# Attention outputs rooted, scaled and turned head by head into the rows of the output product, with two output slabs split early

## The chip, the cores and the metric

One Trainium2 chip, one core, one launch. The metric is the device time in microseconds (us) of the launch. Engines are named as in the profile: PE is the TensorE matmul, PEld its weight load, DVE is VectorE, ACT is ScalarE, POOL is GpSimd, SP is SyncE, whose queue carries the weight loads. A time written 675.2 is a position in the profiled span, in us from its start.

## What is computed

The program is a transformer block followed by two layers of a second kind, on 256 tokens plus 256 context tokens, all float32. In each of the two layers the attention reads:

```python
def diff_attend(q, k, v, lam):
    s = jnp.einsum('bqhcd,bkhcd->bchqk', q, k).astype(jnp.float32) * (ATT_HEAD_DIM ** -0.5)
    p = jax.nn.softmax(s, axis=-1)
    a = p[:, 0] - lam * p[:, 1]
    return jnp.einsum('bhqk,bkhe->bqhe', a.astype(v.dtype), v)
...
def post(o):
    return (rmsnorm(o, subln_g) * (1.0 - lam_init)).reshape(o.shape[0], o.shape[1], ATT_V_DIM)
...
def merge(att, ssd, ga, gs):
    return (jax.nn.sigmoid(ga) * (att @ w_attn_o) + jax.nn.sigmoid(gs) * ssd) @ w_out
```

There are 8 heads of 128 output features. The change concerns `post` (a root mean square over each head of 128, a gain, a constant), the turn of its result from tokens to features, the product `att @ w_attn_o`, and what runs beside it: the step sizes `dt` of the scan (a product of the layer's input with 64 columns of `w_in`, a bias and a softplus) and the sums of `dt * a` over a chunk, from which the scan's decays come.

## The kernel before, in words

**Products in parts.** A float32 product is made as three products of rounded parts: high weights by high input, high weights by low input, low weights by high input. So each slab of weights (128 partitions x 2048 words, 1024 KB, which is 256 output columns by 8 tiles of 128 inputs) is rounded to a high part, and the rest is written over the slab in the ring. In layer 0 POOL does both steps (`split`: L2712 for the high part, L2689 for the rest, each in 4 pieces of 512 words); in layer 1 ACT rounds (`round_slab`, L1368) and POOL takes the rest (`rests`). Both raise `split_ready`, on which PE waits in `split_weights`.

**The ring.** All weights pass a ring of 4 slots. SP issues the loads in the order of use and waits for each until the slab four places earlier has been used (`done[slab - SLOTS]`). Ahead of the output product the ring carries the "mod" slabs (rows of `ada_w`, 1024 KB each, 24 of them in layer 0 and 12 in layer 1), which PE multiplies inside the attention, one per unit at most, where the table `mods_of` puts them (`spread`: over all 32 units of layer 0, over all 16 of layer 1). After the mods come the slab of `dt`, four slabs of `w_attn_o`, and the first slabs of the scan.

**The attention.** A unit is one head and one tile of 128 queries (32 in layer 0, 16 in layer 1; in layer 0 units of 512 and of 256 keys take turns). Per unit u, PE makes the scores of u+2 (L1022), turns the weights of u (L926), makes the outputs of u-1 (L1034) and, where there is one, a mod product (L655). DVE takes the maximum (L2318), scales the outputs of two units before (`out2`, L2339) and mixes the two softmaxes (L2326, L2329, L2333). ACT makes the exponentials (L1611), copies the turned weights (L1465) and squares the outputs, four units behind (L1620).

**After the attention.** ACT takes one root over all heads (L1634); DVE inverts it (L2357), multiplies by `1 - lam_init` (L2359) and scales the outputs, one instruction for each tile of tokens (L2364, 128x1024). Meanwhile PE makes the `dt` product (`to_tokens`, L762: 4 tiles). Then PE turns all 8 heads (L842), with ACT (L1392) and DVE (`rest_of_turned`, L2035) taking the high and the low part of each, and runs a `fill` (L776, matmuls without a result). Then comes the output product, 8 tiles of 128 features (L704, each 8 input tiles by 3 parts = 24 matmuls); behind tiles 4, 5, 6 and 7 PE makes the decay sums of one tile of tokens (`decay_sums`, L1072). DVE multiplies each tile by its gate (`merge`, L2398). ACT and DVE work through the softplus of `dt` beside it (L1654 to L1660, L2370 to L2389); ACT then rounds the first slabs of the scan (`round_of_group(0, q)`, L1651) and takes the exponentials of the decay sums (L1670):

```python
for t in range(TT):
    if t == TT - 1:
        round_of_group(0, 2)
    act.wait_ge(*c.need(dec_ready))
    act.activation(edec[:, t, :], PS[:, 4 + t, 0:192], ACT.Exp)
```

POOL takes the rests of those slabs and then stops at `stage`, where PE, ACT, DVE and POOL wait for one another (`rest_of_group`, L2759; POOL's drain, L2659). Behind it PE begins the scan (L1106).

**To_features by rows.** `to_features` has a form with `row_ready`: its first four tiles (two slabs) are not made one after the other but side by side in four PSUM banks, input tile by input tile ("row" by row), and before each row `row_ready` is called. It is used elsewhere in the kernel.

## Time and profile before

| | us |
|---|---|
| median of 3 runs | 2586.83 (2586.74 to 2587.83) |
| the profiled execution, its own time | 2582.65 |
| its span | 2580.8 |
| PE busy | 2497.3 (97%) |
| POOL busy | 1494.0 (58%) |
| DVE busy | 1217.4 (47%) |
| ACT busy | 1125.7 (44%) |

The profile is of one execution. Its span is the time between the first and the last instruction; the execution's own time has 1.85 us more, and the median of the runs shown is 4.18 us above that. Busy time of one engine may lie beside that of another, so the shares don't add up. The profile's chain of waits is walked back from the last instruction, at each step to what released it.

### The profile page before, as it was taken

The numbers are of one execution on the slowest core, as the hardware profiler recorded it, in microseconds if no ns is written. First come the engines' busy times: TensorE is split into PE (matmuls) and PEld (weight loads), VectorE is DVE, ScalarE is ACT, GpSimd is POOL, SyncE is SP. The second block draws the span as 40 slices with busy tenths as digits, with TensorE's granted clock in tenths as the row PEclk, the third lists the DMA queues.
The fourth block names the chain that finished last, engine by engine and source line by source line (L and its number), as shares of the span: only waits on it lengthen the run. The fifth ranks groups of instructions, "written<-read, shape, count | busy, mean of one in ns | idle before, by whom it ended". The sixth has DMA issues, their size and how long they took to land.

```text
span 2580.8 us, 39739 instructions
## 1 busy us (share of the span) xinstructions
PE 2497.3 (97%) x15548; PEld 2180.7 (84%) x15548; DVE 1217.4 (47%) x2583; ACT 1125.7 (44%) x2371; POOL 1494.0 (58%) x1318
## 2 busy tenths in 40 slices
PE   8999999999999999999999999999989999889999
PEld 7779998985788888888888888889868888889998
DVE  3635502327747888873342112122464888743210
ACT  2445433116527776763032011042465666544532
POOL 1019775860355555544966888854234657656976
PEclk9999999999899999999999999999999999999999
DMA  7566463328432222215323333332544322264564
GB/s 211 195 180 180 127 168 101 95 85 293 157 108 75 58 66 74 58 50 164 98 66 109 94 94 97 97 115 82 183 140 123 91 79 82 77 173 139 184 173 115
DMA packets 388969, 313.03 MB, mean 121 GB/s; under 512 B 12576, under 2 KB 374082, under 8 KB 387778
## 3 DMA queue, kind: packets, MB, share of 16 engines
q1 hardware_dynamic: 385874, 297.75, 39.0%
q10 hardware_dynamic: 2352, 12.59, 1.3%
q8 instruction: 109, 1.79, 0.3%
q0 software_dynamic: 576, 0.43, 0.2%
q14 instruction: 58, 0.48, 0.1%
HBM read 303.40 MB, written 7.34 MB: 120 GB/s over the span
## 4 chain that ended last, share of the span: by engine, by line
PE 72%; POOL 10%; DVE 8%; issue 6%; DMA 2%; ACT 2%; POOLq 1%; SPq 0%; DVEq 0%; ACTq 0%
PE PS L704 34%; POOL rounded L2689 10%; PE PS L1106 10%; PE PS L762 5%; PE PS L1113 3%; PE PS L727 2%; DVE mid_a L2432 2%; PE PS L1234 2%; PE PS L1147 2%; PE PS L655 2%; PE PS L1156 2%; PE PS L1034 1%; PE PS L926 1%; PE PS L1022 1%; DVE mid_v L2486 1%
## 5 line engine op out<-in xcount | busy, mean ns | idle before, releaser
L2689 POOL TENSOR_TENSOR rounded<-ring,rounded 128x512 fp32r<-128x512 f32 (+1 forms) x872 | 1113.1, 1309 | 746.6 <-ACT rounded L1368 424.9
L704 PE MATMUL PS<-rounded 128*128 128x256 f32 (+1 forms) x6864 | 1139.0, 328 | 11.7 <-ACT xT L1758 6.8
L704 PEld LDWEIGHTS PS<-rounded 128*128 128x128 f32 x6864 | 1020.6, 191 | 124.0 <-issue 8.7
L2712 POOL TENSOR_TENSOR rounded<-ring,constants 128x512 fp32r<-128x512 f32 x216 | 229.3, 1092 | 246.9 <-PE PS L704 123.9
L1106 PE MATMUL PS<-rounded 128*128 128x512 f32 (+1 forms) x1536 | 343.5, 380 | 5.6 <-DVE mid_a L2432 5.1
L1106 PEld LDWEIGHTS PS<-rounded 128*128 128x128 f32 x1536 | 275.3, 188 | 60.8 <-DVE mid_a L2432 3.7
L1368 ACT ACTIVATE rounded<-ring 128x2048 fp32r<-128x2048 f32 (+1 forms) x99 | 180.0, 1822 | 150.4 <-DMA ring<-in_w_mlp_dram 55.2
L2432 DVE SCALAR_TENSOR_TENSOR mid_a<-PS,V,mid_a 128x510 f32<-128x510 f32 (+3 forms) x256 | 182.2, 714 | 25.6 <-ACT mid_a L1697 18.1
L1735 ACT ACTIVATE rounded<-constants,big 128x128 fp32r<-128x128 f32 x384 | 150.3, 391 | 0.0
L1735 ACT ACTIVATE rounded<-constants,mid_v 128x128 fp32r<-128x128 f32 x384 | 150.2, 391 | 0.0
L1113 PE MATMUL PS<-rounded 128*128 128x256 f32 x1152 | 147.8, 286 | 0.0
L1113 PEld LDWEIGHTS PS<-rounded 128*128 128x128 f32 x1152 | 142.6, 191 | 1.8
L1907 ACT ACTIVATE PS<-PS 128x512 f32<-128x512 f32 (+1 forms) x64 | 30.4, 475 | 251.4 <-DVE PS L2620 251.3
L2597 DVE SCALAR_TENSOR_TENSOR xT<-PS,mod,xT 128x256 f32<-128x256 f32 x40 | 17.9, 481 | 244.4 <-PE PS L704 244.4
L2620 DVE TENSOR_SCALAR PS<-PS 128x512 f32<-128x512 f32 (+1 forms) x64 | 36.1, 566 | 188.1 <-PE PS L704 177.9
L2469 DVE SCALAR_TENSOR_TENSOR big<-big,by_head 128x128 f32<-128x128 f32 x192 | 106.1, 611 | 18.4 <-POOL big L2790 18.1
L1651 ACT ACTIVATE rounded<-ring 128x1024 fp32r<-128x1024 f32 (+1 forms) x64 | 93.1, 1476 | 32.0 <-DMA ring<-in_w_in_dram 32.0
L762 PE MATMUL PS<-rounded 128*128 128x256 f32 x768 | 102.7, 290 | 0.0
L2305 DVE TENSOR_TENSOR edec<-PS,constants 128x256 f32<-128x256 f32 x32 | 13.6, 425 | 179.1 <-PE PS L1006 178.8
L762 PEld LDWEIGHTS PS<-rounded 128*128 128x128 f32 x768 | 96.4, 191 | 1.8
L727 PE MATMUL PS<-rounded 128*128 128x256 f32 (+1 forms) x480 | 87.0, 341 | 5.7 <-DVE rounded L2041 4.0
L727 PEld LDWEIGHTS PS<-rounded 128*128 128x128 f32 x480 | 75.1, 191 | 17.4 <-DVE rounded L2041 3.8
(263 smaller groups left out, 3114.5 us busy)
## 6 DMA issues: line engine op xcount, KB each, us to landing
ring<-in_w_mlp_dram SPq DMA_DIRECT2D x64, 1024.0 KB, 5.6
ring<-in_w_in_dram SPq DMA_DIRECT2D x56, 1024.0 KB, 5.3
ring<-in_ada_w_dram SPq DMA_DIRECT2D x48, 1024.0 KB, 5.2
ring<-in_w_in_dram SPq DMA_DIRECT2D x81, 512.0 KB, 4.1
ring<-in_w_up_dram SPq DMA_DIRECT2D x44, 512.0 KB, 5.1
ring<-in_w_ssd_o_dram SPq DMA_DIRECT2D x16, 1024.0 KB, 5.8
ring<-in_w_out_dram SPq DMA_DIRECT2D x12, 1024.0 KB, 5.1
ring<-in_w_down_dram SPq DMA_DIRECT2D x16, 704.0 KB, 4.9
```

The lines of the kernel that those rows point to most:

```text
L704: mm = pe.matmul(PS[:, b, 0:cols], w[:, k, m * P:(m + 1) * P], x(half * kt + k), start=(half == 0 and k == 0 and n_pass == 0), stop=(half ...
L727: mm = pe.matmul(PS[:, b, 0:cols], w[:, k, m % 2 * P:(m % 2 + 1) * P], x(k), start=(k == 0 and n_pass == 0), stop=(k == kt - 1 and n_pass ...
L762: mm = pe.matmul(PS[:, b, 0:width], x[:, k, t * P:(t + 1) * P], w[:, k, :], start=(k == 0 and n_pass == 0), stop=(k == KT - 1 and n_pass = ...
L1106: mm = pe.matmul(PS[:, b, 0:cols], w[:, k, m:m + P], x[:, k, 0:cols], start=(k == 0 and x is hs_hi and w is w_hi), stop=(k == KT - 1 and w ...
L1113: mm = pe.matmul(PS[:, b, t * GW:(t + 1) * GW], x[:, k, t0:t0 + P], w[:, k, :], start=(k == 0 and x is hs_hi and w is w_hi), stop=(k == KT ...
L1368: act.activation(view(R, at[n % len(at)], size), ring[:, slab % SLOTS, 0:size], ACT.Copy)\
L1651: act.activation(view(R, group_hi(s, q), words), ring[:, s, 0:words], ACT.Copy).then_inc(*c.made(round_ready))
L1735: act.activation(seg_parts[d][n][:, r * P:(r + 1) * P], mask, ACT.Copy, scale=dta_parts[n][:, t, h:h + 1]).then_inc(*c.made(seg_in))
L2432: ins = dve.scalar_tensor_tensor(out=cv[:, :, to], in0=u[:, :, fr], scalar=V[:, bass.ds(g * st + (cw + 32 * (d + 2) + off), 1)], in1=cv[:, ...
L2469: step(dve.scalar_tensor_tensor(out=m, in0=cb_lo[:, t, :], scalar=dt[:, t, g * GH + r:g * GH + r + 1], in1=m, op0=ALU.mult, op1=ALU.add))
L2689: ins = pool.tensor_tensor(lo[:, r], raw[:, r], hi[:, r], ALU.subtract)
L2712: ins = pool.tensor_tensor(hi[:, r], raw[:, r], ones[:, 0:1].broadcast_to([P, 512]), ALU.mult)
```

## The change

- **Roots.** ACT takes the root in two parts: over the first 7 heads in layer 0 (6 in layer 1) in the last unit of the attention, over the rest after it (`roots_of_heads`). The factor `1 - lam_init` is multiplied into the gain once, at the start.
- **Scaling and turning by head.** DVE scales head by head over all tiles of tokens (`scale_head`, 128x512 in layer 0, 128x256 in layer 1): heads 0 and 1 before the outputs of the last unit, each later head ahead of the low part of the head two before. PE turns heads 0 and 1 and then makes the first four tiles of the output product side by side (`row_ready=head_row`): before row f it turns head f+2 and waits for the low part of head f.
- **dt.** The `dt` product is made behind these four tiles (`between`), and its slab is loaded between the second and the third slab of `w_attn_o`. All four decay sums move behind the last two tiles: t=0 and 1 behind tile 6, t=2 and 3 behind tile 7.
- **Mods.** The mod products are spread over the first 26 of the 32 units of layer 0 and the first 13 of the 16 of layer 1.
- **Slabs.** In layer 0 POOL splits the first two slabs of `w_attn_o` inside the attention, as soon as they are loaded, into memory of their own (`split_into`). In layer 1 ACT rounds them in units 14 and 16, the third after the turned heads, the fourth behind the first four `hs_hi` copies (L1658).
- **DVE.** `merge` of the first four tiles comes ahead of the softplus, the other four behind it, each with two rests of `hs_lo`.

```diff
+        out_at = [[AT["big2"] + KT * T, AT["big2"] + KT * T + SLAB], mix_at[1][0:2]]
...
-        mods_of = [spread(len(UNITS1), 0, EARLY), spread(len(units2(0)), EARLY, LATE + EARLY),
-                   spread(len(units2(1)), 2 * EARLY + LATE, LATE)]
+        mods_of = [spread(len(UNITS1), 0, EARLY), spread(len(units2(0)) - 6, EARLY, LATE + EARLY),
+                   spread(len(units2(1)) - 3, 2 * EARLY + LATE, LATE)]
+        rooted_first = [HEADS - 1, HEADS - 2]
...
+                first_slab["attn_o", l] = len(done)
+                wide(of_layer("w_attn_o_2", l), 0, 2)
                 slabs(1, KT, 64, lambda j: wi[:, :, C_DT:C_DT + 64], lambda j: TT * j)
-                first_slab["attn_o", l] = len(done)
-                wide(of_layer("w_attn_o_2", l), 0, 4)
+                wide(of_layer("w_attn_o_2", l), 512, 2)
...
-                pe.wait_ge(*c.need(o_done))
-                ring_begin(dve_freed)
-                to_tokens(1, 64, TT, dve_freed)
-                pe.wait_ge(*c.need(tok_scaled, n_tok))
-                turn_begin()
-                for f in range(KT):
-                    turn([o2[:, t, f * P:(f + 1) * P] for t in range(n_tok)])
-                fill(3, tile[0] % 4)
-                turn_end()
+                def turn_head():
+                    f = heads_turned[0]
+                    if f == KT:
+                        return
+                    heads_turned[0] += 1
+                    if f == 1:
+                        pe.wait_ge(*c.need(o_done))
+                    pe.wait_ge(*c.need(tok_scaled))
+                    turn([o2[:, t, f * P:(f + 1) * P] for t in range(n_tok)], ring=False)
+
+                def head_row():
+                    turn_head()
+                    pe.wait_ge(*c.need(turned_freed))
                 def decay_sums(n):
-                    t = n - 4
-                    if t < 0:
+                    if n < 6:
                         return
-                    if t == 0:
+                    if n == 6:
                         pe.wait_ge(*c.need(dta_ready))
+                    for t in (2 * n - 12, 2 * n - 11):
...
+                for _ in range(2):
+                    turn_head()
                 to_features(4, lambda k: att_hi[l][:, k, :], q_cols, dve_freed, rest=lambda k: att_lo[l][:, k, :],
-                            hi_at=mix_at[l], after=decay_sums, begin=False)
+                            hi_at=mix_at[l], after=decay_sums, row_ready=head_row, first_at=out_at[l],
+                            between=lambda: to_tokens(1, 64, TT, dve_freed))
...
+                    if u == n_u - 1:
+                        roots_of_heads(0, rooted_first[l])
+                    if l and u in (n_u - 2, n_u):
+                        round_slab(slabs, 16 + (u - n_u + 2) // 2, mix_at[l])
-                act.activation(stat[:, 224:224 + ny * HEADS], stat[:, 192:192 + ny * HEADS], ACT.Sqrt, scale=1.0 / P,
-                               bias=eps[:, 0:1]).then_inc(*c.made(tok_rms))
-                if l:
-                    for n in range(16, 20):
-                        round_slab(slabs, n, mix_at[l])
+                roots_of_heads(rooted_first[l], HEADS)
                 for f in range(KT):
                     turned_to(att_hi[l][:, f, :], q_cols, col("attn_subln_g_2", l), hi_ready)
+                if l:
+                    round_slab(slabs, 18, mix_at[l])
...
                 for k in range(KT // 2):
                     act.activation(hs_hi[:, k, :], hT[:, k, :], ACT.Copy).then_inc(*c.made(hi_ready))
+                if l:
+                    round_slab(slabs, 19, mix_at[l])
                 act.wait_ge(*c.need(dt_one))
...
+                    if u == n_u + 1:
+                        roots_taken(0, rooted_first[l])
+                        for f in range(2):
+                            scale_head(f)
-                for t in range(ny):
-                    h = o2[:, t, :].rearrange("p (h e) -> p h e", h=HEADS)
-                    dve.tensor_tensor(h, h, bc(stat[:, 192 + t * HEADS:192 + (t + 1) * HEADS], P), ALU.mult)\
-                        .then_inc(*c.made(tok_scaled))
+                for f in range(2, KT):
+                    if f == rooted_first[l]:
+                        roots_taken(f, HEADS)
+                    scale_head(f)
+                    rest_of_head(f - 2)
+                for f in range(KT - 2, KT):
+                    rest_of_head(f)
+                for n in range(4):
+                    merge(n)
...
-                for n in range(KT):
-                    merge(n)
-                    rest_of(hs_lo[:, n, :], hT[:, n, :], hs_hi[:, n, :])
+                for n in range(4):
+                    merge(4 + n)
+                    for k in (2 * n, 2 * n + 1):
+                        rest_of(hs_lo[:, k, :], hT[:, k, :], hs_hi[:, k, :])
...
+                    a0 = first_slab["attn_o", l]
+                    pool.wait_ge(*slab_used[s0 + 15])
+                    for n in range(2):
+                        split_into(a0 + n, out_at[l][n])
                     pool.wait_ge(*c.need(o_done, len(units2(l))))
-                    split(range(a0, a0 + 4), mix_at[l])
+                    for n in range(2):
+                        split_into(a0 + 3 + n, mix_at[l][n])
...
-                    rests(range(a0, a0 + 4), mix_at[l])
+                    rests([a0, a0 + 1, a0 + 3, a0 + 4], mix_at[l])
```

## Rows read from the trace of the kernel before

**Rows 1.** The page, part 1: busy time, share, instructions.
```profile
PE 2497.3 (97%) x15548; PEld 2180.7 (84%) x15548; DVE 1217.4 (47%) x2583; ACT 1125.7 (44%) x2371; POOL 1494.0 (58%) x1318
```

**Rows 2.** Timeline of PE, layer 0: start, extent, group, idle before it.
```profile
675.62 12.63 PE L762 MATMUL PS<-ring,hT 128*128 128x64 f32 x64 [0.44 <-DVE mid_o L2339]
...
695.66 27.51 PE L704 MATMUL PS<-rounded 128*128 128x512 f32 x120 [0.68 <-DVE rounded L2035]
...
737.26 5.74 PE L704 MATMUL PS<-rounded 128*128 128x512 f32 x24
742.84 1.22 PE L1072 MATMUL PS<-by_head,constants 128*128 128x32 f32 x10
...
746.31 18.90 PE L1106 MATMUL PS<-rounded 128*128 128x512 f32 x82 [0.15 <-POOLq L2659]
```

**Rows 3.** Windows: stretch, busy PE, PEld, DVE, ACT, POOL, granted clock, DMA, GB/s.
```profile
677.00:690.60 13.60, 13.60 (x67) 13.60 (x67) 12.06 (x12) 1.92 (x4) 13.52 (x10) 0.50 0.09 27
1916.00:1922.80 6.80, 3.90 (x14) 3.24 (x15) 3.42 (x8) 6.52 (x11) 6.80 (x6) 0.51 0.01 2
```

**Rows 4.** Timeline of PE, layer 1.
```profile
1903.60 7.36 PE L762 MATMUL PS<-ring,hT 128*128 128x64 f32 x64 [0.45 <-DVE mid_o L2339]
1910.80 1.04 PE L842 MATMUL PS<-constants,mid_o 128*128 128x128 f32 x8
1918.90 1.97 PE L842 MATMUL PS<-constants,mid_o 128*128 128x128 f32 x8 [7.06 <-DVE rounded L2035]
...
1922.87 14.77 PE L704 MATMUL PS<-rounded 128*128 128x256 f32 x120
...
1949.43 1.22 PE L1072 MATMUL PS<-by_head,constants 128*128 128x32 f32 x10
...
1955.28 13.00 PE L1106 MATMUL PS<-rounded 128*128 128x512 f32 x56 [0.38 <-POOLq L2659]
```

**Rows 5.** Timeline of PE in the attention of layer 0: turned weights of units.
```profile
595.33 0.66 PE L926 MATMUL PS<-constants,big 128*128 128x128 f32 x4 [0.50 <-DVE big L2333]
...
601.32 0.66 PE L926 MATMUL PS<-constants,big 128*128 128x128 f32 x4
...
606.87 0.66 PE L926 MATMUL PS<-constants,big 128*128 128x128 f32 x4 [0.50 <-DVE big L2333]
...
667.27 0.44 PE L926 MATMUL PS<-constants,big 128*128 128x128 f32 x2
...
672.62 0.44 PE L926 MATMUL PS<-constants,big 128*128 128x128 f32 x2 [0.36 <-DVE big L2333]
```

**Rows 6.** Timeline of POOL, layer 0: one slab's high part; another's rest.
```profile
675.64 4.03 POOL L2712 TENSOR_TENSOR rounded<-ring,constants 128x512 fp32r<-128x512 f32 x4 [109.85 <-DVE mid_o L2339]
...
692.63 5.00 POOL L2689 TENSOR_TENSOR rounded<-ring,rounded 128x512 fp32r<-128x512 f32 x4
```

**Rows 7.** The instructions of line L2364 (DVE): duration ns min/median/max.
```profile
L2364 DVE TENSOR_TENSOR mid_o<-mid_o,stat x6: 1218/2144/2286, 678.7 to 1907.3; 128x1024 f32<-128x1024 f32 x6
```

**Rows 8.** Timeline of DVE, attention of layer 0.
```profile
669.35 0.75 DVE L2333 SCALAR_TENSOR_TENSOR big<-big,stat 128x512 f32<-128x512 f32 x1
```

**Rows 9.** The page, part 6: issues, KB each, us from issue to landing.
```profile
ring<-in_ada_w_dram SPq DMA_DIRECT2D x48, 1024.0 KB, 5.2
```

**Rows 10.** Timeline of ACT, layer 0, at the last tiles of the output product.
```profile
737.49 0.33 ACT L1670 ACTIVATE edec<-PS 128x192 f32<-128x192 f32 x1 [6.28 <-PE PS L1072]
737.72 1.91 ACT L1651 ACTIVATE rounded<-ring 128x2048 fp32r<-128x2048 f32 x1
```

**Rows 11.** The chain of waits, layer 0: POOL's last rest and its drain.
```profile
739.67 6.60 POOLq L2659
```

**Rows 12.** Timeline of ACT, layer 1: table load of the root; softplus.
```profile
1904.00 1.28 ACT L1634 ACT_TABLE_LOAD   x1
...
1921.28 0.41 ACT L1654 ACTIVATE big<-big 128x256 f32<-128x256 f32 x1
...
1923.33 2.18 ACT L1658 ACTIVATE rounded<-hT 128x512 fp32r<-128x512 f32 x4
```

More of the change, by code:

```diff
@@ L672, in to_features @@
                             rest=None, hi_at=None, lo_at=None, after=None, row_ready=None, first_at=(None, None), aside=4, first_rows=None,
-                            begin=True, end=True, held=None, last_rows=None):
+                            begin=True, end=True, held=None, last_rows=None, between=None):
                 if begin:
@@ L735, in to_features @@
                     side_by_side()
+                    if between:
+                        between()
                     for j in range(aside // 2, 4):
@@ L1052, in _ @@
                 c.skip(p_ready, 4)
[L1053 to L1055 removed]
                 n_tok = len(y_chunks(l))
[L1057 to L1062 removed]
+                heads_turned = [0]
@@ L1073, in decay_sums @@
-                    mm.then_inc(*c.made(dec_ready))
+                    for t in (2 * n - 12, 2 * n - 11):
+                        for m, lhs, r0, w in ((0, t_gt, 0, 32), (32, t_le, 0, 32), (64, t_lt, 32, 32), (96, t_ge, 32, 32),
+                                              (128, ones, 0, 64)):
+                            mm = pe.matmul(PS[:, 4 + t, m:m + w], lhs, dta[:, t, r0:r0 + w], start=True, stop=True)
+                        mm.then_inc(*c.made(dec_ready))
+                for _ in range(2):
+                    turn_head()
@@ L1548, in _ @@
                 a0 = first_slab["attn_o", l]
-                slabs = [*range(s0, s0 + 16), *range(a0, a0 + 4)]
+                slabs = [*range(s0, s0 + 16), a0, a0 + 1, a0 + 3, a0 + 4]
                 if l == 0:
@@ L1621, in sum_squares, with roots_of_heads @@
                                    accum_out=stat[:, 192 + t * HEADS + h:193 + t * HEADS + h]).then_inc(*c.made(act_step))
+                def roots_of_heads(h0, h1):
+                    act.wait_ge(*c.sofar(act_step))
+                    roots, sums = (stat[:, at:at + ny * HEADS].rearrange("p (t h) -> p t h", h=HEADS)[:, :, h0:h1]
+                                   for at in (224, 192))
+                    act.activation(roots, sums, ACT.Sqrt, scale=1.0 / P, bias=eps[:, 0:1]).then_inc(*c.made(tok_rms))
                 n_u = len(units)
@@ L2128, in _ @@
             step(dve.tensor_scalar(q_gain, q_gain, HD ** -0.5, None, ALU.mult))
+            for l in range(LAYERS):
+                g = col("attn_subln_g_2", l)
+                step(dve.tensor_scalar(g, g, 1.0 - (0.8 - 0.6 * float(np.exp(-0.3 * l))), None, ALU.mult))
             settle()
@@ L2340, in out2, with roots_taken, scale_head, rest_of_head @@
                                       ALU.mult).then_inc(*c.made(o_done))
+                def roots_taken(h0, h1):
+                    dve.wait_ge(*c.need(tok_rms))
+                    rstd, roots = (stat[:, at:at + ny * HEADS].rearrange("p (t h) -> p t h", h=HEADS)[:, :, h0:h1]
+                                   for at in (192, 224))
+                    step(dve.reciprocal(rstd, roots))
+                    settle()
+                def scale_head(f):
+                    h = o2[:, 0:ny, f * P:(f + 1) * P]
+                    settle(o_done)
+                    dve.tensor_tensor(h, h, bc(stat[:, 192 + f:192 + ny * HEADS:HEADS], P), ALU.mult)\
+                        .then_inc(*c.made(tok_scaled))
+                def rest_of_head(f):
+                    rest_of_turned(att_lo[l][:, f, :], att_hi[l][:, f, :], col("attn_subln_g_2", l), q_cols)
                 mods = mods_of[1 + l]
@@ L2727, in split, with split_into @@
                     split_slabs.extend(slabs[2 * body:])
+            def split_into(slab, hi_at):
+                s = slab % SLOTS
+                pool.wait_ge(*slab_loaded[slab])
+                raw, hi = ring[:, s, :], view(R, hi_at, SLAB)
+                for r in in_pieces(SLAB):
+                    ins = pool.tensor_tensor(hi[:, r], raw[:, r], ones[:, 0:1].broadcast_to([P, 512]), ALU.mult)
+                ins.then_inc(*c.made(pool_step))
+                pool.wait_ge(*c.sofar(pool_step))
+                rest_in_place(s, hi_at, AT["ring"] + s * SLAB, SLAB)
             def first_rests(slabs, at):
```

35 lines of the change are left out of this document (11 added, 24 removed).

## The prediction, made before the changed kernel was run

> **What bounds the kernel now.** The page's first part: PE is busy for 97% of the span [rows 1], so whatever lengthens or shortens PE's own sequence shows in the time, and the question is what PE does and waits for between the last unit of the attention and the scan, once per layer. I read PE's timeline there, then the windows for its clock, then who releases it.
>
> Layer 0 [rows 2]: the outputs end at 675.2, the `dt` product takes 12.63 us, turns and fill follow, the output product begins at 695.66, its last tile ends at 743.0 (737.26 + 5.74), the last decay sum begins at 742.84 and the scan at 746.31. The `dt` product and most of the turns ran at a granted clock of 0.50, which is 1.2 of 2.4 GHz, from 677.0 to 690.6 [rows 3]: the same 64 matmuls take 7.36 us in layer 1, at full clock [rows 4]. Layer 1 loses otherwise: PE stands for 7.06 us before the last turns, since ACT waits for a slab, and then works at the low clock until 1922.8 [rows 3, 4].
>
> **The attention gets longer.** *Mods forward.* A pair of units with two mod products takes 5.99 us (595.33 to 601.32), with one 5.55 us (to 606.87) [rows 5]. The last units are bound by the exchange with DVE: 5.35 us a pair (667.27 to 672.62) though mods are in it, so those mods are free. The first 28 units take 7 x (5.99 + 5.55) = 80.8 us now; with 24 mods in them 12 x 5.99 + 2 x 5.35 = 82.6. That is +1.8 us; the last four stay. In layer 1, where I take the same effect on 12 mods, +0.4.
>
> *POOL beside DVE.* POOL was idle for 109.85 us before it began its first output slab at 675.64 [rows 6]. Now it splits two slabs while the units run. A slab is free when mod 20 (then 21) is done, at about 649, and lands 5.2 us later [rows 9], so POOL starts at about 654.5 and is busy for 2 x (4.03 + 5.00) = 18.1 us, about 21 with DVE's share. The six scalings of L2364 show the price for DVE: both inputs in SBUF, 1.22 us at the least, 2.14 in the median [rows 7]; the long ones are those of layer 0, beside POOL. They stood back to back and each paid about 1.0, the length of one POOL instruction (4.03/4) [rows 6]. The Trainium skill, page "SBUF — State Buffer", section "Who interferes with whom", says that a VectorE instruction with two SBUF inputs and a GpSimd one that reads SBUF exclude each other for the whole instruction, and that issue order decides who blocks; by that alone the second of two VectorE instructions in a row could be free. The rows say it is not, and I go by them. Each unit has two such instructions on its path, L2329 and L2333 (0.75 us alone [rows 8]). The first comes at a random moment and waits half an instruction, 0.55; the second waits a whole one, 1.0 to 1.25. So 1.6 us a unit, bounds 0 and 2.2. A unit is 2.7 us without it, 4.3 with it: 21/4.3 = 4.9 units, 7.8 us, less 0.3 of slack where mods remain: +7.5 us.
>
> *The root's table load* (1.28 us [rows 12]) now stands ahead of the last copy of turned weights on ACT, which had about a us of slack: +0.3. Layer 0's attention ends 9.6 us later.
>
> **Layer 0, from the last outputs to the last tile.** Now 67.8 us (675.2 to 743.0) [rows 2]. Then: DVE inverts the first roots and scales two heads ahead of the outputs of the last unit, ACT squares, roots and takes head 0, DVE takes its low part; from rows of their kind some 4.0 us, with PE turning three heads in it, until row 0. Eight rows are 96 matmuls of 27.51/120 = 0.229 us [rows 2], 22.0 us, and five turns of four transposes at 1.04/8 = 0.13 us [rows 4], 2.7. DVE needs per row about 1.8 us (a scaling, a low part), ACT 0.7, so PE is not held. The clock: the low stretch now begins behind the same thin end of the attention, and rows would begin in it: I take 2.5 us, between 0 and 5. Then the first merge, 0.7, `dt` at full clock 7.4, tiles 4 and 5 11.0, tile 6 5.5, two decay sums 2.4, tile 7 5.5. Sum 63.7 us: -4.1. Hidden here: the fourth slab (its slot falls free at the end of the rows, landing 5.2, split 9.0, needed 19 us after the rows) and the softplus (ready some 9 us behind `dt`, needed at 22).
>
> **From the last tile to the scan.** This is the change's surest cost. The third slab of the scan is rounded on ACT behind the exponential of t=2. That decay sum came behind tile 6, and the rounding at 737.72 lay beside tile 7 [rows 10]. Now t=2 and t=3 both come behind tile 7. Behind ACT's rounding stands POOL's rest of it, and behind that the stop at which all four engines wait: 6.60 us in layer 0 [rows 11]. From the begin of the first decay sum: its extent of 1.22 [rows 2] to the exponential, 0.23 from there to the rounding, 1.91 for it [rows 10], then 5.6 to 6.6: 9.0 to 10.0, I take 9.6 where there are 3.5 (742.84 to 746.31) [rows 2]: +6.1. PE runs out of work some 5 us before, so the scan may begin at the low clock: +1.0, between 0 and 2.
>
> Layer 0: 9.6 - 4.1 + 6.1 + 1.0 = +12.6 us.
>
> **Layer 1.** The attention ends 2.2 us later (0.4 for mods; 1.8 as ACT's rounding of slab 16 and POOL's rest stand before the last units' weights). ACT rounds slab 17 behind the last copy; its rest is done 5.8 us after the last outputs, and row 0 needs it in its second half. Rows: 0.7 + 7 x 12 x 0.123 (14.77/120) + 5 x 0.27 = 12.4. Merge and `dt` 7.8. Tiles 4 and 5 take 5.9, but the fourth slab is late: ACT rounds it behind the softplus's exponential and four copies. From the end of `dt`: 0.6 until ACT begins, 4.2 until the four copies end (1921.28 to 1925.51) [rows 12], 1.9 for the rounding, 5.2 for the rest: 12.0 to 12.4. So PE waits 6.3 us, much as it waits 7.06 now [rows 4], and pays for the clock, 1.3. Then 2.95 + 2.05 + 2.95. The last decay sums begin 47.7 us after the last outputs; now 46.3 (1903.2 to 1949.43): +1.4. To the scan 9.1 where there are 5.85 [rows 4]: +3.3. Layer 1: 2.2 + 1.4 + 3.3 = +6.9 us.
>
> The gain multiplied once at the start is two instructions of about 0.2 us beside loads, and L2359 twice less: nothing.
>
> **Sum.** +19.5 us on the profiled execution's 2582.65, and the median stands 4.18 above that: 2606 us.
>
> **The rivals.**
> *DVE goes first half the time.* If only the first of the two instructions waits (0.55 a unit, about 6 units), the attention's +7.5 is 3.0: 2602 us. The skill's sentence on issue order speaks for it; the back-to-back scalings [rows 7] speak against it.
> *The low clock spreads.* Without mods the end of the attention is thinner than what stood before 677.0 [rows 3]. If `dt` also ran at the low level (12.63 for 7.36, +5.3) and the rows lost 3 more: 2614 us.
> *POOL stays hidden: faster.* Everything that costs hangs on POOL: its share of the attention (7.5), the rest before the stop (6.1 + 3.3, and 1.0 of clock), the rests of slabs 17 and 19 (about 3.4 + 6.3 + 1.3). Together 28.9. If PE never found POOL late, the time would be 2577 us; the change is faster from the point at which more than 20 of these are hidden. For it: ACT and POOL are idle for much of the stretch, and the 5.3 us of low clock in `dt` and the 7.06 us stop of layer 1 go in any case. Against it: the order on ACT is fixed, and t=2 can't come before tile 7.
> *In between*: two thirds of that hidden, about 2587 us, no difference that is measured.
> That the head-by-head order doesn't overlap at all is not likely: DVE's 1.8 us per row stands against PE's 3.3.
>
> **How the numbers follow.** A difference of 0.2% (5.2 us) is about what a measurement of this kernel tells from none. Forecast 0.55; DVE first 0.20; clock spreads 0.11; POOL hidden 0.07; in between 0.07. So faster 0.07, same 0.07, slower 0.86. The range: below, the attention's mods and lock at nothing and the clock terms gone (1.8 + 7.5 + 1.0 + 1.3 less) give 2594; above, the third case and a wait of 2.2 a unit give 2616.
>
> **What would show it.** PE's timeline: the last outputs of layer 0 near 685, `dt` in 7.4 us at a clock of 1.0, some 10 us from the last decay sums but one to the scan in both layers with a release by POOL's drain; in layer 1 a wait before tile 6 of about 6 us, released by POOL's rest. L2329 and L2333 at up to 1.3 and 1.9 us in five units. The forecast is wrong if L2333 keeps its 0.75 us, if slab 19 is ready when tile 5 ends, or if the rounding of the scan's third slab ends before tile 7 does.

## The result and the profile after

The changed kernel takes 2602.47 us (median of 5, 2598.7 to 2607.32), the kernel before 2586.83 on the same chip: a measured ratio of 1.0068, 95% interval 1.0057 to 1.0080 (the two medians alone give 1.0060, inside the interval). It is slower by 15.6 us by the medians, by 17.6 by the ratio, where 2606 was forecast and 2594 to 2616 was the range. The profiled execution took 2601.43 us, its span 2599.6.

The timeline of PE in the changed kernel, layer 0 (start, extent, line, group, idle before it and what ended it):

```profile
688.08 1.92 PE L848 MATMUL PS<-constants,mid_o 128*128 128x128 f32 x8
...
691.16 1.20 PE L730 MATMUL PS<-rounded 128*128 128x512 f32 x4
...
715.46 7.25 PE L767 MATMUL PS<-ring,hT 128*128 128x64 f32 x64
722.51 16.62 PE L707 MATMUL PS<-rounded 128*128 128x512 f32 x72
...
741.12 5.74 PE L707 MATMUL PS<-rounded 128*128 128x512 f32 x24
746.70 2.34 PE L1086 MATMUL PS<-by_head,constants 128*128 128x32 f32 x20
...
756.80 9.56 PE L1123 MATMUL PS<-rounded 128*128 128x512 f32 x30 [5.66 <-POOLq L2706]
```

Against [rows 2]: the last outputs end at 688.3 instead of 675.2. From there to the end of the last tile it is 58.6 us (to 746.86) instead of 67.8: the rows begin 2.9 us behind the outputs, and `dt` takes 7.25 us at full clock where it took 12.63. Then PE stands for 5.66 us, and the scan begins 10.1 us after the begin of the last decay sums (746.70), where it was 3.5.

The same in layer 1:

```profile
1915.29 0.69 PE L932 MATMUL PS<-constants,big 128*128 128x128 f32 x4 [3.10 <-DVE big L2363]
...
1918.23 1.59 PE L1040 MATMUL PS<-mid_v,big 128*128 128x128 f32 x8 [0.54 <-DVE mid_o L2369]
...
1924.24 0.98 PE L730 MATMUL PS<-rounded 128*128 128x256 f32 x6 [1.17 <-POOL rounded L2736]
...
1936.20 7.26 PE L767 MATMUL PS<-ring,hT 128*128 128x64 f32 x64
1943.27 5.99 PE L707 MATMUL PS<-rounded 128*128 128x256 f32 x48
1955.56 5.15 PE L707 MATMUL PS<-rounded 128*128 128x256 f32 x24 [6.30 <-POOL rounded L2736]
...
1965.64 2.34 PE L1086 MATMUL PS<-by_head,constants 128*128 128x32 f32 x20
...
1974.27 10.95 PE L1123 MATMUL PS<-rounded 128*128 128x512 f32 x47 [2.03 <-POOLq L2706]
```

The 7.06 us in which PE stood before the last turns [rows 4] are gone, and a wait of 6.30 us for POOL stands before tile 6 instead. Ahead of the turned weights of the last unit PE now waits 3.10 us.

The windows of the changed kernel over three stretches at the low level of TensorE's clock (columns as in [rows 3]): the last unit and the first turned heads, the begin of the scan, tile 6 of layer 1.

```profile
680.00:690.50 10.50, 7.26 (x30) 6.21 (x30) 5.71 (x13) 5.70 (x18) 1.64 (x2) 0.51 0.00 0
755.00:762.00 7.00, 5.20 (x12) 4.18 (x13) 0.63 (x2) 2.62 (x4) 2.65 (x4) 0.52 0.00 0
1953.30:1960.20 6.90, 4.64 (x22) 4.64 (x23) 6.83 (x8) 3.80 (x5) 6.90 (x6) 0.51 0.19 45
```

Why the attention of layer 0 is longer is seen on DVE beside POOL. The timeline of DVE, its two instructions per unit, in the changed kernel:

```profile
657.94 0.22 DVE L2359 SCALAR_TENSOR_TENSOR stat<-stat,neg_lam 128x1 f32<-128x1 f32 x1
658.20 1.42 DVE L2363 SCALAR_TENSOR_TENSOR big<-big,stat 128x512 f32<-128x512 f32 x1
...
668.57 0.49 DVE L2359 SCALAR_TENSOR_TENSOR stat<-stat,neg_lam 128x1 f32<-128x1 f32 x1
669.10 1.23 DVE L2363 SCALAR_TENSOR_TENSOR big<-big,stat 128x256 f32<-128x256 f32 x1
...
680.10 0.75 DVE L2363 SCALAR_TENSOR_TENSOR big<-big,stat 128x512 f32<-128x512 f32 x1
```

and POOL's two early slabs:

```profile
658.01 4.50 POOL L2782 TENSOR_TENSOR rounded<-ring,constants 128x512 fp32r<-128x512 f32 x4 [88.27 <-DMA ring<-in_w_attn_o_dram]
...
668.01 4.21 POOL L2782 TENSOR_TENSOR rounded<-ring,constants 128x512 fp32r<-128x512 f32 x4
672.30 5.38 POOL L2736 TENSOR_TENSOR rounded<-ring,rounded 128x512 fp32r<-128x512 f32 x4
```

From 658.0 to 677.7, and only then, L2363 is at 1.23 to 1.72 us for 0.75 (512 elements) and 0.48 (256): six of them, 5.0 us over. L2359 is at 0.22 to 0.72, 0.8 us over in all.

Cut into segments, by PE's first and last instruction of each (us of the profiled execution; "begin" is the code ahead of the second attention, the same in all kernels but for two short DVE instructions of the gain; e1 to e10 are the experiments below):

| | begin | attention 0 | to scan | to layer 1 | attention 1 | to scan | rest |
|---|---|---|---|---|---|---|---|
| before | 579.0 | 96.1 | 71.1 | 1098.3 | 58.5 | 52.1 | 625.6 |
| changed | 583.0 | 105.3 | 68.5 | 1100.9 | 62.2 | 54.5 | 625.4 |
| e1 | 580.8 | 105.3 | 62.5 | 1100.0 | 62.6 | 52.1 | 629.3 |
| e2 | 584.7 | 105.5 | 68.5 | 1100.7 | 62.4 | 47.7 | 622.9 |
| e3 | 585.0 | 99.1 | 87.1 | 1100.4 | 63.1 | 55.6 | 626.2 |
| e4 | 580.3 | 103.5 | 71.1 | 1100.0 | 58.5 | 52.1 | 625.6 |
| e5 | 582.4 | 105.4 | 62.5 | 1099.6 | 62.1 | 49.6 | 627.3 |
| e6 | 584.2 | 103.5 | 69.0 | 1100.3 | 63.1 | 55.4 | 627.3 |
| e7 | 583.2 | 98.0 | 72.3 | 1099.7 | 59.3 | 52.4 | 625.7 |
| e8 | 581.3 | 100.3 | 63.8 | 1099.8 | 62.1 | 49.6 | 627.9 |
| e9 | 580.1 | 101.3 | 63.8 | 1100.5 | 61.4 | 50.7 | 624.3 |
| e10 | 581.4 | 104.7 | 69.0 | 1100.9 | 59.3 | 63.4 | 630.6 |

The first column differs by 6 us between executions in which nearly the same instructions run, and the last by 7.7: in these stretches the granted clock falls to its low level at other places each time. The segments between repeat better, though not fully: where the code of a segment is the same, attention 0 took 104.7 to 105.5 us (changed, e1, e2, e5, e10) and 100.3 and 101.3 (e8, e9), and the way from the scan to layer 1 took 1098.3, 1100.0 and 1099.7 (before, e4, e7). Without the first column, the changed kernel is longer by 9.2 - 2.6 + 2.5 + 3.7 + 2.3 - 0.2 = 14.9 us, near what the medians show (15.6). Of it, the 2.5 us in the way to layer 1 are not far over that spread.

### The profile page after: what moved, and what is told of

It is laid out like the page before. It is cut to its first block, busy times and chain, and to the rows that moved or that the text cites. A ratio compares the mean times of both kernels' runs of the same rounds, so it can differ in the third digit from the quotient of the medians.

```text
span 2599.6 us, 39733 instructions
## 1 busy us (share of the span) xinstructions
PE 2496.1 (96%) x15536; PEld 2177.4 (84%) x15536; DVE 1236.0 (48%) x2595; ACT 1125.7 (43%) x2373; POOL 1491.0 (57%) x1318
## 4 chain that ended last, share of the span: by engine, by line
PE 70%; POOL 10%; DVE 9%; issue 6%; ACT 2%; DMA 1%; POOLq 1%; SPq 0%; DVEq 0%; ACTq 0%
PE PS L707 33%; POOL rounded L2736 10%; PE PS L1123 9%; PE PS L767 4%; PE PS L730 3%; PE PS L1130 3%; DVE mid_a L2479 3%; PE PS L1251 2%; PE PS L658 2%; PE PS L1164 2%; PE PS L1173 2%; PE PS L1028 1%; PE PS L1040 1%; PE PS L932 1%; DVE mid_v L2533 1%
## 5 line engine op out<-in xcount | busy, mean ns | idle before, releaser
L1123 PEld LDWEIGHTS PS<-rounded 128*128 128x128 f32 x1536 | 277.2, 189 | 68.5 <-POOLq L2706 8.5
L2759 POOL TENSOR_TENSOR rounded<-ring,constants 128x512 fp32r<-128x512 f32 x200 | 212.2, 1091 | 127.2 <-PE PS L707 114.0
L2335 DVE TENSOR_TENSOR edec<-PS,constants 128x256 f32<-128x256 f32 x32 | 13.6, 425 | 179.1 <-PE PS L1012 178.8
```

The costliest lines, as they stand in the source:

```text
L1123: mm = pe.matmul(PS[:, b, 0:cols], w[:, k, m:m + P], x[:, k, 0:cols], start=(k == 0 and x is hs_hi and w is w_hi), stop=(k == KT - 1 and w ...
L2759: ins = pool.tensor_tensor(hi[:, r], raw[:, r], ones[:, 0:1].broadcast_to([P, 512]), ALU.mult)
```

## The experiments

My theory is that of the forecast: the attention pays for POOL beside DVE, and the way to the scan for ACT's order. Ratios are to the kernel before on the same chip, with 95% intervals. A ratio's interval is 2 to 5 us to either side, so the totals tell two experiments apart by some 4 to 6 us, and below that the segments decide. No kernel here leaves out a part of the computation.

**e1: the scan's third slab rounded one exponential earlier.**

```diff
-                    if t == TT - 1:
+                    if t == TT - 2:
                         round_of_group(0, 2)
```

> The changed kernel with one line altered: the third slab of the scan is rounded on ACT ahead of the exponential of t=2 instead of behind it, so ahead of the wait for the last decay sums. Theory (what stands before the scan is ACT's rounding and POOL's rest behind it, both held back by a decay sum that now comes behind the last tile): the way from the first of the last decay sums to the scan falls from 10.1 us to about 3.5 in layer 0 and from 8.6 to about 5.7 in layer 1, the low clock at the start of the scan (2.8 us) goes too, and the time falls by 9 to 12 us against the changed kernel, to about 2591 to 2593, that is 1.002 of the kernel before. Rival (POOL is late for another reason, its drain, and ACT's order is a bystander): the scan begins as late as now and the time stays within 2 us of 2602.

Ratio 1.0049 (1.0032 to 1.0065), 2597.56 us. PE's timeline at the scan of layer 0, then at that of layer 1:

```profile
744.52 2.34 PE L1086 MATMUL PS<-by_head,constants 128*128 128x32 f32 x20
...
748.60 3.56 PE L1123 MATMUL PS<-rounded 128*128 128x512 f32 x14
...
1957.05 2.34 PE L1086 MATMUL PS<-by_head,constants 128*128 128x32 f32 x20
...
1963.29 3.10 PE L1123 MATMUL PS<-rounded 128*128 128x512 f32 x12
```

The scan begins 4.1 us and 6.2 us after the begin of the last decay sums (10.1 and 8.6 in the changed kernel), without a wait. So ACT's order was what held POOL: 6.0 us in layer 0 and 2.3 in layer 1, as the segments say. The total fell by less than the expected 9 us, by about 5; the profiled execution took 3.9 us more than the changed kernel's in the rest (mean granted clock 0.98 there, 0.99 in the changed kernel), which this line doesn't touch, and the two intervals together leave some 5 us open either way.

**e2: the fourth output slab of layer 1 rounded ahead of the softplus.**

```diff
                 if l:
                     round_slab(slabs, 18, mix_at[l])
+                    round_slab(slabs, 19, mix_at[l])
...
-                if l:
-                    round_slab(slabs, 19, mix_at[l])
```

> The changed kernel with ACT's rounding of the fourth output slab of layer 1 moved ahead of the softplus and its copies, right behind that of the third. Theory: POOL's rest of it begins some 11 us earlier, PE's wait of 6.3 us ahead of tile 6 in layer 1 goes, and with it the low clock of that tile (about 2 us); against it stand up to 1.9 us in which the softplus is later, which the two tiles behind dt hide. So 7.5 us less than the changed kernel, about 2595, 1.003 of the kernel before. Rival (the slab's arrival bounds, not its rounding, or PE then waits for the later softplus): under 3 us gained, 2599 or more.

Ratio 1.0035 (1.0022 to 1.0047), 2594.34 us. PE's timeline in layer 1:

```profile
1938.82 7.25 PE L767 MATMUL PS<-ring,hT 128*128 128x64 f32 x64
1945.89 8.87 PE L707 MATMUL PS<-rounded 128*128 128x256 f32 x72
...
1963.96 4.15 PE L781 MATMUL PS<-constants 128*128 128x256 f32 x18 [1.81 <-DVE mid_a L2417]
1969.50 2.79 PE L1123 MATMUL PS<-rounded 128*128 128x512 f32 x11 [1.40 <-DVEq L1985]
```

and ACT's rounding of that slab:

```profile
1943.57 1.91 ACT L1385 ACTIVATE rounded<-ring 128x2048 fp32r<-128x2048 f32 x1 [6.59 <-DMA ring<-in_w_attn_o_dram]
```

The wait of 6.30 us is gone: three tiles in one piece. 6.8 us of the segment go, and 8.5 of the total by the ratios (0.0033 x 2587), known to some 4 us. The rounding was pulled forward less than I had thought: ACT now waits 6.59 us for the slab to land, and begins 4.7 us behind the begin of `dt` (1938.82 to 1943.57), where it was 12.0 in the changed kernel (1936.20 to 1948.22). The 1.81 us before the fill are not the softplus: PE waits there for DVE's last merge (L2417), and the two-input instructions between the merges (L2067) take 3.10 to 3.15 us a pair beside POOL's rest of a scan slab, where a pair takes 1.28 in the changed kernel. The scan itself is now released by DVE (1.40 us), not by POOL.

**e3: POOL's early slabs behind the outputs again.**

```diff
                     pool.wait_ge(*slab_used[s0 + 15])
+                    pool.wait_ge(*c.need(o_done, len(units2(l))))
                     for n in range(2):
                         split_into(a0 + n, out_at[l][n])
-                    pool.wait_ge(*c.need(o_done, len(units2(l))))
```

> The changed kernel with POOL's two early output slabs of layer 0 moved back behind its wait for the outputs, so that nothing runs on POOL beside the attention. Theory (of the 9.2 us by which the attention of layer 0 is longer, some 7 are DVE waiting for POOL): the attention of layer 0, from its first scores to its last outputs, takes 98 us where the changed kernel takes 105.3 and the kernel before 96.1, and L2363 is never over 1.0 us in it. The rows then wait for POOL: row 0 cannot begin before about 18 us behind the last outputs, so the total is longer than the changed kernel's, by 5 to 10 us, about 2610. Rival (the attention is longer through its mods and the order on PE, not through POOL): it stays at 103 us or more.

Ratio 1.011 (1.0093 to 1.0127), 2614.74 us. The attention takes 99.1 us, and L2363 is back at its own duration. The instructions of that line over the end of the attention, and PE behind it:

```profile
L2363 DVE SCALAR_TENSOR_TENSOR big<-big,stat x15: 485/485/752, 639.5 to 679.4; 128x256 f32<-128x256 f32 x8, 128x512 f32<-128x512 f32 x7
```

```profile
695.65 2.90 PE L730 MATMUL PS<-rounded 128*128 128x512 f32 x6 [9.29 <-POOL rounded L2736]
704.55 2.93 PE L730 MATMUL PS<-rounded 128*128 128x512 f32 x6 [6.00 <-POOL rounded L2736]
```

So 6.2 of the 9.2 us come with POOL's early slabs; the waits of L2363 and L2359 add up to 5.8 of them. The rest may be clock: the attention's last 8.1 us were at the low level in the changed kernel (from 680.2 on), the last 5.0 in e3 (from 679.1 on). Without the early split PE waits 15.3 us around row 0, whose matmuls then run at the low clock: starting POOL early is worth its price in this order of work. The total is 11 us above the changed kernel's by the ratios, a little over the 5 to 10 expected.

**e4: the kernel before with 16 instructions on POOL that nobody waits for.**

```diff
+                    pool.wait_ge(mod_ready, EARLY + 19)
+                    for n in range(16):
+                        there = view(R, AT["big2"] + KT * T + SLAB, 512)
+                        if n % 8 < 4:
+                            ins = pool.tensor_tensor(there, K[:, 0:512], ones[:, 0:1].broadcast_to([P, 512]), ALU.mult)
+                        else:
+                            ins = pool.tensor_tensor(there, K[:, 0:512], K[:, 512:1024], ALU.subtract)
+                        ins.then_inc(*c.made(pool_step))
+                        pool.wait_ge(*c.sofar(pool_step))
                     pool.wait_ge(*c.need(o_done, len(units2(l))))
```

> The kernel before, with 16 instructions of 512 elements added on POOL while the attention of layer 0 runs, of the same two kinds and in the same order as those that split two slabs, but on constants and into a place that nobody reads: its output is unchanged, and nothing waits for them but POOL's own output slabs, long after. Theory (DVE's instructions with two inputs in SBUF wait for a whole POOL instruction): the attention of layer 0 is longer by about 7.5 us (4.9 units by 1.6), and the total by 5 to 8 us, about 2593. Rival (the lock hits the first of two instructions by half a POOL instruction): 3 us, about 2590. Second rival (DVE's waits are hidden behind PE and ACT): 0 to 1 us.

Ratio 1.0034 (1.0020 to 1.0048), 2594.07 us. The attention takes 103.5 us for 96.1, 7.3 more, and the segments to the scans and the attention of layer 1 stay within 0.1 us of those before. The total is some 9 us longer by the ratio, over the 5 to 8 expected. DVE's timeline, the kernel before plus POOL's load:

```profile
658.81 1.01 DVE L2329 SCALAR_TENSOR_TENSOR stat<-stat,neg_lam 128x1 f32<-128x1 f32 x1
659.85 1.62 DVE L2333 SCALAR_TENSOR_TENSOR big<-big,stat 128x512 f32<-128x512 f32 x1
...
664.12 1.19 DVE L2329 SCALAR_TENSOR_TENSOR stat<-stat,neg_lam 128x1 f32<-128x1 f32 x1
665.35 1.57 DVE L2333 SCALAR_TENSOR_TENSOR big<-big,stat 128x256 f32<-128x256 f32 x1
...
669.87 0.22 DVE L2329 SCALAR_TENSOR_TENSOR stat<-stat,neg_lam 128x1 f32<-128x1 f32 x1
670.12 1.60 DVE L2333 SCALAR_TENSOR_TENSOR big<-big,stat 128x512 f32<-128x512 f32 x1
```

Two measurements by opposite routes (POOL taken out of the changed kernel, 6.2 us; POOL put into the kernel before, 7.3) give nearly one price. Both hold some of the clock: in e4 the low level lay in these very units (666.4 to 673.2, granted clock 0.50). DVE's waits alone, summed over L2329 and L2333, are 5.6 us in four units in e4, against 5.8 in six in the changed kernel. The rival in which the first instruction alone pays is out: where the first pays nothing, the second pays 0.85 (1.60 for 0.75), and where the first pays 0.97 (1.19 for 0.22) the second pays 1.09 again. The Trainium skill, page "SBUF — State Buffer", section "Who interferes with whom", says that issue order decides who blocks; these rows show that the DVE instruction behind one that has waited is not ahead in that order.

**e5: e1 and e2 together.**

> The changed kernel with both of ACT's roundings forward: the third slab of the scan ahead of the exponential of t=2, and the fourth output slab of layer 1 right behind the third. Theory: the two act in different places and add up. The first alone took 4.7 us off the changed kernel, the second 8.0, so some 12.5 us together: 2589 to 2590, 1.002 of the kernel before. Segment by segment: last outputs to scan 62.5 us in layer 0 and about 46 in layer 1 (54.5 in the changed kernel). Rival (in layer 1 both waited in line for one and the same thing, POOL): the sum falls short by the 2.3 us that the first was worth in layer 1.

Ratio 1.0009 (1.0000 to 1.0018), 2587.75 us (11 runs). Two lines in ACT's order take back 15 of the 17.6 us (0.0068 x 2587) that the change cost. In layer 0 the segment is 62.5 us, as expected. In layer 1 it is 49.6, not 46, and not even the 47.7 of e2: there the rival holds. The scan begins 9.7 us after the begin of the last decay sums (1951.85 to 1961.55), the same 9.7 as in e2 (1959.81 to 1969.50), where e1 alone had 6.2. PE again waits for the last merge, 1.81 us, with DVE's instructions before it at 3.1 us a pair beside POOL, so e1's line frees nothing there. More of this execution also lay at the low clock: 1908.6 to 1922.3, for 3.4 us in the changed kernel and 10.2 in e2. The totals can't tell this 2 us from their interval.

**e6: the early slabs in pieces of 256 elements.**

```diff
-                for r in in_pieces(SLAB):
-                    ins = pool.tensor_tensor(hi[:, r], raw[:, r], ones[:, 0:1].broadcast_to([P, 512]), ALU.mult)
+                for r in in_pieces(SLAB, width):
+                    ins = pool.tensor_tensor(hi[:, r], raw[:, r], ones[:, 0:1].broadcast_to([P, width]), ALU.mult)
...
-                        split_into(a0 + n, out_at[l][n])
+                        split_into(a0 + n, out_at[l][n], 256)
```

> The changed kernel with POOL's two early output slabs of layer 0 split in pieces of 256 elements instead of 512, so twice as many instructions of half the length. Theory (a DVE instruction waits for the whole of the POOL instruction that has begun): a wait is about 0.5 us where it is 1.0, the attention of layer 0 takes about 102 us where the changed kernel takes 105.3, and L2363 is at 1.2 at most. The total is 3 us less, 2599. Rival (the wait has a length of its own, or DVE waits until POOL is done with several): the attention stays at 105 us or more and the total does not move.

Ratio 1.0057 (1.0042 to 1.0073), 2600.84 us. DVE's timeline:

```profile
666.07 1.18 DVE L2363 SCALAR_TENSOR_TENSOR big<-big,stat 128x512 f32<-128x512 f32 x1
669.25 0.92 DVE L2363 SCALAR_TENSOR_TENSOR big<-big,stat 128x256 f32<-128x256 f32 x1
```

and one slab on POOL:

```profile
670.71 5.06 POOL L2782 TENSOR_TENSOR rounded<-ring,constants 128x256 fp32r<-128x256 f32 x8
675.85 6.14 POOL L2736 TENSOR_TENSOR rounded<-ring,rounded 128x256 fp32r<-128x256 f32 x8
```

L2363 waits 0.31 to 0.55 us in seven units, where it was 0.67 to 0.97 in six: the wait goes with the length of POOL's instruction. But POOL needs 22.6 us for the two slabs instead of 19.6, so more units meet it, and the attention gains 1.8 us, not 3. The total (2.8 us less by the ratios) alone can't tell this from no gain.

**e7: the kernel before with the mods moved alone.**

```diff
-        mods_of = [spread(len(UNITS1), 0, EARLY), spread(len(units2(0)), EARLY, LATE + EARLY),
-                   spread(len(units2(1)), 2 * EARLY + LATE, LATE)]
+        mods_of = [spread(len(UNITS1), 0, EARLY), spread(len(units2(0)) - 6, EARLY, LATE + EARLY),
+                   spread(len(units2(1)) - 3, 2 * EARLY + LATE, LATE)]
```

> The kernel before with nothing but the placing of the mod products changed to that of the changed kernel: none beside the last six units of the attention of layer 0 and the last three of layer 1. Theory: attention of layer 0 longer by 1.8 us (mods are free in the last units, where the exchange with DVE bounds), of layer 1 by 0.4: the total 2 us longer than the kernel before, 2587. Of the 3.0 us by which the attention stays longer when POOL does not run beside it, this would be the larger part. Rival (the thin end lowers the clock): a longer stretch at 0.5 behind the last outputs and 4 to 6 us more.

Ratio 1.0019 (1.0009 to 1.0028), 2589.91 us. The attentions take 98.0 and 59.3 us: +1.85 and +0.8. The total is 4.9 us longer by the ratio (2.3 to 7.2), not 2. The rival is there in part: the low stretch behind the outputs lasts 17.1 us where it lasted 13.6 [rows 3], and the segment to the scan is 1.1 us longer.

```profile
680.10:697.20 17.10, 16.66 (x78) 16.36 (x79) 11.46 (x13) 2.89 (x7) 15.49 (x11) 0.50 0.03 7
```

**e8: e5 and e6, with two of layer 0's mods in the last units.**

```diff
-                   spread(len(units2(0)) - 6, EARLY, LATE + EARLY),
+                   {**spread(26, EARLY, 22), 28: EARLY + 22, 30: EARLY + 23},
```

> The changed kernel with both roundings forward, the early slabs of layer 0 split in pieces of 256, and the mod products of layer 0 placed as 22 beside the first 26 units and two beside units 28 and 30. Theory: on top of 2589.5 for the roundings alone, 3 us less for the shorter waits of DVE and 1 to 2 us less for mods that are free at the end: about 2585, within 0.1% of the kernel before. Rival (the early slabs, 7 us later now, come too late for row 0): PE waits for POOL at the first row, and the time is 2589 or more.

Ratio 1.0004 (0.9995 to 1.0013), 2586.94 us (10 runs). The attention of layer 0 takes 100.3 us, 5.1 less than in e5, and the low stretch at its end is not there (granted clock 1.0 over the whole of it); in e6, with the same pieces and the mods as in the changed kernel, it was (10.2 us from 681.3). Behind it, 1.3 us are given back: POOL is done at 685.73 and row 0 begins at 685.76. The profile puts PE's last 0.54 us of waiting to DVE's low part of head 0, which began at 684.96, so both come just in time.

**e10: layer 1, the rounding of the first output slab two units later** (told ahead of e9, on which it bears).

```diff
-                    if l and u in (n_u - 2, n_u):
-                        round_slab(slabs, 16 + (u - n_u + 2) // 2, mix_at[l])
+                    if l and u == n_u:
+                        for n in (16, 17):
+                            round_slab(slabs, n, mix_at[l])
```

> The changed kernel with ACT's rounding of the first output slab of layer 1 moved two units back, to stand right ahead of that of the second, so that nothing but the root stands between the last exponentials and no rest of POOL runs beside the last weights. Theory (of the 3.65 us by which the attention of layer 1 is longer, 0.8 are mods, and most of the rest is this rounding ahead of the last exponentials together with DVE's wait for POOL's rest): the attention of layer 1 takes about 59.5 us where the changed kernel takes 62.2, the last L2363 is back at 0.75 us. The rows then stand until both rests are done, 5 us later than now, so the total is 2 to 4 us more. Rival (the table load of 1.28 us is what holds the last unit): the attention of layer 1 stays above 61 us.

Ratio 1.0082 (1.0064 to 1.0100), 2609.98 us. The attention of layer 1 takes 59.3 us, the figure of e7 with mods alone, and the last of DVE's mixing instructions (L2363 in the changed kernel, 1.72 us there beside POOL) is back at 0.75. So its +3.65 are 0.8 of mods and 2.85 of this rounding, with DVE's wait for POOL behind it; the table load for the root costs nothing. The rows then wait 3.16 and 3.73 us for POOL and run at the low clock at first. By the ratios the total is 3.6 us more than the changed kernel's (known to some 5 us), as expected; the two segments of layer 1 together are 6.1 us longer.

```profile
1920.75 1.62 PE L730 MATMUL PS<-rounded 128*128 128x256 f32 x6 [3.16 <-POOL rounded L2737]
1926.10 1.65 PE L730 MATMUL PS<-rounded 128*128 128x256 f32 x6 [3.73 <-POOL rounded L2737]
```

**e9: e8, with layer 1 mended too.**

```diff
-                   spread(len(units2(1)) - 3, 2 * EARLY + LATE, LATE)]
+                   spread(len(units2(1)), 2 * EARLY + LATE, LATE)]
...
                     if u < n_u:
                         exp2(u)
+                    if l and u == n_u - 1:
+                        round_slab(slabs, 16, mix_at[l])
...
-                    if l and u in (n_u - 2, n_u):
-                        round_slab(slabs, 16 + (u - n_u + 2) // 2, mix_at[l])
+                    if l and u == n_u:
+                        round_slab(slabs, 17, mix_at[l])
```

> The kernel of e8 with two edits in layer 1: ACT rounds the first output slab behind the exponentials of the last unit instead of ahead of them, and the mod products are spread over all 16 units as in the kernel before. Theory (the last unit of layer 1 is held by ACT: 1.9 us of rounding ahead of its exponentials, and PE waits 3.1 us for its weights): the attention of layer 1 falls from 62.1 us to about 60, the stretch behind it loses some low clock, and the total is 2 to 3 us less than e8's, 2584, 0.9995 of the kernel before. Rival (the 1.9 us only move to the copy of turned weights behind it, and the table load for the root still stands there): the attention of layer 1 stays above 61.5 us and the total at 2587.

Ratio 0.9996 (0.9987 to 1.0004), 2584.04 us against 2586.27 (12 runs). The total came as expected, its cause only in part: the attention of layer 1 fell by 0.7 us to 61.4, near the rival's bound, and the segment behind it rose by 1.2, since the second half of row 0 now waits 2.0 us for POOL. In the profiled execution the rest was shorter by 3.6 us (mean granted clock 0.99 for 0.98), in stretches that these edits don't touch, so what of the 2.9 us between e8 and e9 is theirs stays open. No version beats the kernel before by more than a measurement tells: the best stands level with it.

## Why the prediction was right

Its direction and its time held (2606 for 2602.5). By its steps:

- **Attention of layer 0**, +9.6 forecast, +9.2 measured. *Mods* +1.8, measured 1.85 alone (e7). *POOL beside DVE* +7.5, measured 6.2 (e3) and 7.3 (e4). The product was right, its factors were not: I took 4.9 units at 1.6 us, there were 6 at about 1.0. The short first instruction, which I let wait for half an instruction of POOL, waits for nothing worth naming in four of the six units (0.22 to 0.26; the others 0.49 and 0.72), and the second for 0.67 to 0.97 rather than 1.0 to 1.25; as each unit is shorter, more of them meet POOL. *Table load* +0.3: e10 shows none in layer 1, and in layer 0 ACT, done with load and root at 684.58, still stood 0.32 us until PE had the last turned weights, so it cost nothing there either. About 1 us is left; the low clock in the last units is the likely place, not shown alone.
- **Last outputs to last tile, layer 0**, 63.7 us forecast, 58.6 measured. This was the largest error, 5.1 us too high. The rows began after 2.9 us and not 4.0; the low clock of 2.5 us in the rows wasn't there, since the low stretch (680.2 to 690.4) lay in the last units and the first heads; the first merge (0.7) was hidden; rows, `dt`, tiles and decays took some 0.8 less together (rows 24.3 for 24.7, `dt` 7.25 for 7.4). The order of work held; the place of the low clock did not, and the margins were too wide.
- **To the scan, layer 0**, +6.1 forecast, +6.6 measured, released by POOL's drain as the text said; e1 takes it away with one line. The low clock at the scan's begin was put at 1.0 (0 to 2): from the scan to layer 1 the changed kernel takes 2.5 us more than before, but only 0.9 more than e1, whose scan begins without the wait, and e4 and e7, with the code of before, take 1.6 and 1.3 more than before. In those three a second low stretch of 3.4 us stands further on in the segment (at 1130.7 in e4), which neither the kernel before nor the changed one has. So the cost lies between 0.9 and 2.5 us, and one execution of each doesn't tell it closer.
- **Layer 1.** Attention +2.2 forecast, +3.65 measured: mods 0.8 for 0.4, rounding and rest 2.85 for 1.8 (e7, e10). Last outputs to last decay sums 47.7 forecast, 45.8 measured (1919.82 to 1965.64), with the wait before tile 6 at 6.30 for 6.3. To the scan 9.1 forecast, for which the forecast gives no working, 8.6 measured. The terms printed for the way to the last decay sums add up to 47.45, not 47.7, which changes nothing. That slab's cause was told right (ACT's order) but not in full: e2 shows its landing as the next bound, and behind it DVE's merges, late through the two-input instructions between them.
- **The sum**: 19.5 forecast, 14.9 by the segments, 15.6 by the medians. The largest single error is the 5.1 us of layer 0's rows above; layer 1's attention, 1.45 too low, goes against it, and the other errors are smaller, so part of the agreement of the total is errors that cancel.

**The rivals.** "DVE first half the time" gave 2602, nearest to what came, for a reason that is not so: it let only the first of the two instructions wait, and the runs show the second waiting in every unit beside POOL, with a cost near the forecast's (6.2 us in e3, 7.3 in e4). "The low clock spreads" fell: `dt` ran at 1.0 in both layers. "POOL stays hidden" is what e1, e2 and e5 make by hand: with most of those terms hidden but the attention's share, the time is level with before, the 2587 of the case in between.

## What to carry to other kernels

When work is made finer so that an engine can start on it earlier, look at what else is queued by count behind the same events: here two exponentials that came one by one now came together behind the last tile, and a rounding that stood between them moved with them onto the critical path; e1 takes back 6.0 us in layer 0 and 2.3 in layer 1. Price a GpSimd instruction that is moved beside a chain of VectorE by the number of two-input VectorE instructions it will meet, and each wait at somewhat less than the GpSimd instruction's length (0.67 to 1.09 us beside instructions of 1.05 to 1.43); shorter pieces lower the single wait and raise the number. The same price came back where ACT's order was mended: POOL's rests, now earlier, stood beside the two-input instructions between DVE's merges (e2, e5). And compare kernels by segments: two profiled executions differed by up to 6 us in code that was the same.

## What the runs showed that I had not expected

- A one-element VectorE instruction (L2359, L2329: 0.22 us) takes up to 1.01 and 1.19 us beside POOL in e4, but waits less than 0.05 us in six of the ten units of e4 and the changed kernel; the long one right behind it paid 0.67 us or more in all ten.
- Splitting POOL's instructions in two cost 0.2 us for each one more: 5.06 us for 8 of 256 elements (e6), 4.21 for 4 of 512 (changed kernel), both beside DVE.
- The granted clock falls to 0.5 in code that is the same in every kernel, and not at the same place in each execution: at 148.0 in the profile of the kernel before, at 332.0 and 390.0 in that of the changed kernel. The attention of layer 0 began between 579.0 and 585.0 us.
- With two mods beside the last units the low stretch at the end of layer 0's attention was gone (e8 and e9, one profiled execution each), and with none there (e7) it grew from 13.6 to 17.1 us.
- Where two edits were each worth something in layer 1 (e1 2.3 us, e2 6.8), both together gave no more than e2 alone (49.6 us for 47.7): another engine, DVE, had become the last to be done.
